# Second attention of a two-block transformer kernel: units of a head pair and a query half, matmuls that alternate between halves of the array, distances and maximum in one vector operation

## What is computed

```
N_HEADS, N_KV_HEADS, HEAD_DIM, WINDOW, BLOCK = 16, 4, 64, 128, 128
def sliding_window_attention(h, w_qkv, b_qkv, sinks, w_o, b_o):
    qkv = h @ w_qkv + b_qkv
    ...
    kb, vb = with_prev(k), with_prev(v)          # the block before and the own block
    scores = einsum("bnqgrd,bnkgd->bngrqk", q, kb) * HEAD_DIM ** -0.5
    dist = qi + BLOCK - kj
    valid = (dist >= 0) & (dist < WINDOW) & (key_pos >= 0)
    scores = where(valid, scores - slopes * dist, -inf)
    m = maximum(max(scores, -1), sink)
    p = exp(scores - m)
    probs = p / (sum(p, -1) + exp(sink - m))
    out = einsum("bngrqk,bnkgd->bnqgrd", probs, vb)
    return out.reshape(B, S, Q_DIM) @ w_o + b_o
```

## Time and profile before

| | |
|---|---|
| median of three runs | 2310.18 us |
| span of the profiled execution | 2305.6 us |
| median less span (no time of its own is listed for the profiled execution beside its span) | 4.6 us |
| TensorE busy | 2259.3 us, 98% |
| VectorE, GpSimd, ScalarE busy | 1151.5, 1049.4, 1000.7 us |
| second attention, first logits to the stage's tail | 132.64 us |
| granted TensorE clock in it | 1.00 |

### The profile page before, as it was taken

How to read it: one execution, slowest core, us unless ns; L and a number is a source line. 1 busy time by engine, 2 the same in 40 slices (tenths; PEclk the granted TensorE clock), 3 DMA queues, 4 the chain that set the end, 5 groups by cost and what they waited for, 6 DMA issues and landing times.

```text
span 2305.6 us, 28989 instructions
## 1 busy us (share of the span) xinstructions
PE 2259.3 (98%) x11624; PEld 1883.2 (82%) x11624; DVE 1151.5 (50%) x1766; ACT 1000.7 (43%) x1888; POOL 1049.4 (46%) x794
## 2 busy tenths in 40 slices
PE   7999999999999999999999999999999999999998
PEld 4788777778988888888888888878888889888887
DVE  4877787746522123377573335451543456724353
ACT  4765567654533224555552222463332236322234
POOL 2544443446444445522354454544354344544543
PEclk9999999999999999999999999999999999999999
DMA  6222233465232222311222222322222222232221
GB/s 281 92 84 100 89 134 126 163 216 186 75 110 92 92 106 90 121 41 38 74 92 99 98 96 92 110 92 92 78 105 92 92 92 74 92 109 82 101 103 62
DMA packets 42662, 239.79 MB, mean 104 GB/s; under 512 B 5024, under 2 KB 7072, under 8 KB 17184
## 3 DMA queue, kind: packets, MB, share of 16 engines
q1 hardware_dynamic: 40096, 232.28, 28.0%
q10 hardware_dynamic: 2432, 5.66, 0.8%
HBM read 226.38 MB, written 8.39 MB: 102 GB/s over the span
## 4 chain that ended last, share of the span: by engine, by line
PE 79%; DVE 11%; ACT 6%; POOL 2%; issue 1%; DMA 1%; ACTq 0%; DVEq 0%; SPq 0%; POOLq 0%
PE PS L739 78%; DVE DD L1881 2%; POOL WL L2622 1%; DVE TG L1887 1%; DVE HLO L1887 1%; DVE SQ L1887 1%; DVE PS L1887 1%; ACT WH L1309 1%; DVE X L1881 1%; DVE SCT L2204 1%; PE PS L1157 1%; DVE VV L1884 0%; DVE SB L2258 0%; ACT SB L1635 0%; DVE T L1881 0%
## 5 line engine op out<-in xcount | busy, mean ns | idle before, releaser
L2622 POOL TENSOR_TENSOR WL<-RAW,WH 128x512 fp32r<-128x512 f32 (+1 forms) x688 | 921.3, 1367 | 1122.0 <-ACT WH L1309 1105.0
L739 PE MATMUL PS<-HHI,WH 128*128 128x512 f32 x1488 | 595.4, 400 | 1.5 <-DVE GB L1887 1.4
L739 PE MATMUL PS<-HHI,WL 128*128 128x512 f32 x1488 | 580.6, 390 | 0.0
L739 PE MATMUL PS<-HLO,WH 128*128 128x512 f32 x1488 | 580.1, 390 | 0.0
L1309 ACT ACTIVATE WH<-RAW 128x512 fp32r<-128x512 f32 (+1 forms) x688 | 378.3, 613 | 394.7 <-PE PS L739 375.8
L739 PEld LDWEIGHTS PS<-HHI,WH 128*128 128x128 f32 x1488 | 279.8, 188 | 74.1 <-issue 12.6
L739 PEld LDWEIGHTS PS<-HHI,WL 128*128 128x128 f32 x1488 | 279.5, 188 | 59.4
L739 PEld LDWEIGHTS PS<-HLO,WH 128*128 128x128 f32 x1488 | 280.0, 188 | 56.6 <-issue 2.2
L739 PE MATMUL PS<-UF,WH 128*128 128x512 f32 (+1 forms) x832 | 224.0, 357 | 0.0
L1881 DVE TENSOR_TENSOR T<-PS,R 128x512 f32<-128x512 f32 x112 | 76.9, 690 | 217.8 <-PE PS L739 209.9
L739 PEld LDWEIGHTS PS<-UF,WH 128*128 128x128 f32 x832 | 148.3, 189 | 22.8
(11 more groups left out here) (357 smaller groups left out, 3574.7 us busy)
## 6 DMA issues: line engine op xcount, KB each, us to landing
RAW<-in_wts SPq DMA_DIRECT2D x190, 1024.0 KB, 4.9
FW<-in_wts SPq DMA_DIRECT2D x6, 1024.0 KB, 17.4
spill<-T SPq DMA_DIRECT2D x24, 256.0 KB, 3.4
RAW<-in_wts SPq DMA_DIRECT2D x8, 768.0 KB, 4.1
GT<-spill SPq DMA_DIRECT2D x20, 256.0 KB, 4.3
X<-in_xt SPq DMA_DIRECT2D x2, 1024.0 KB, 9.2
out_x<-X SPq DMA_DIRECT2D x8, 256.0 KB, 2.3
X<-in_xt SPq DMA_DIRECT2D x2, 768.0 KB, 9.0
```

Of the source, the lines that this page charges most:

```text
L739: return e.matmul(o_, l, r, start=start, stop=stop)
L2622: return e.tensor_tensor(o_, a, b, f)
```

## The change

A unit u is now head pair k = u // 2 and query half u % 2 (blocks 0 and 1, or 2 and 3), for both heads of the pair, i = 0 and 1. There are again 16 units, and the two buffers, banks and turns are used as before.

- Logits: for each block and each part the matmul of head i = 0 (partitions 0-63, bank 0) is followed by that of head i = 1 (partitions 64-127, bank 1). Block 0's missing previous block is left out, so an even unit has 6 matmuls and an odd one 8.
- Values: likewise i = 0 (output partitions 0-63) and i = 1 (64-127) in turn, 6 or 8 matmuls.
- Queries are scaled by -1 / (8 slope), `QUERY[h]` = -2^((h+1)/2 - 3), when their bias is added (a new constant qf; bq is multiplied by it once), so that one table of distances, DW [256], serves all heads. One `tensor_tensor_reduce` per head and block adds DW, scales and takes the maximum: four of 128x256, or two of 128x256 and two of 128x128 in an even unit. The sinks are negated once; one small operation gives the negative maximum, a second the exponent of the sink, `sink2`.
- Order on TensorE: logits of h+1, values of h-2, transposes of h-1, the pieces of `ROUNDS[h]`; values of 15 after the loop. The copies out of bank 4 and into O2 move one turn later too.

The core of the diff:

```diff
-        def logits2(h):
-            g, r0 = h // 4, 64 * (h % 2)
...
+        def logits2(u):
+            k, g = u // 2, u // 4
...
+            for nn in range(2):
+                n = 2 * (u % 2) + nn
+                for part, kb in ((0, n - 1), (1, n)):
+                    for i in range(2):
+                        if kb >= 0:
+                            r, c0 = slice(64 * i, 64 * i + 64), 256 * nn + 128 * part
+                            t = mm(PS[:, i, c0:c0 + 128], Q2[r, k, 128 * n:128 * n + 128], K2[r, g, 128 * kb:128 * kb + 128], True, True)
...
+                    for i in range(2):
+                        if kb >= 0:
+                            t = mm(PS[64 * i:64 * i + 64, 4, 128 * n:128 * n + 128], V2[:, kb, 64 * g:64 * g + 64],
+                                   PT[:, 4 * part + 2 * nn + i, :], part == 0 or n == 0, part == 1)
...
         for h in range(17):
-            n = len(ROUNDS[h])
+            if h < 15:
+                logits2(h + 1)
+            if h > 1:
+                values2(h - 2)
             if h:
                 turn2(h - 1)
-            if h < 15:
-                logits2(h + 1)
-                n = 0
-            for s in ROUNDS[h][:n]:
+            for s in ROUNDS[h]:
                 rows2(*s)
-            if h:
-                values2(h - 1)
-            for s in ROUNDS[h][n:]:
-                rows2(*s)
+        values2(15)
...
-                e.activation(Q2[:, k, :], Q2[:, k, :], ACT.Identity, bias=v("bq", k)).then_inc(*up("a_mix", ("q2", k)))
+                q.wait_ge(*at(("bq",)))
+                e.activation(Q2[:, k, :], Q2[:, k, :], ACT.Identity, scale=v("qf", k), bias=v("bq", k)).then_inc(*up("a_mix", ("q2", k)))
...
-            stt(S[:, :, :], DW[:, :, :], -8.0 * 2.0 ** (-8.0 * (h + 1) / 16), pv, MUL, ADD).then_inc(*up("d_ev", ("logits2_ev", h)))
-            q.wait_ge(*at(("logits2_ev", h)))
-            e.reduce_max(C2(h, 0), S[:, :, :], AX).then_inc(*up("d_mix", ("max2", h)))
...
+            for i in range(2):
+                for nn in range(2):
+                    s, lo = 2 * nn + i, 128 if u % 2 == 0 and nn == 0 else 0
+                    t = e.tensor_tensor_reduce(S[:, s, lo:256], PS[:, i, 256 * nn + lo:256 * nn + 256], DW[:, lo:256],
+                                               1.0 / QUERY[u // 2 * 2 + i], -1e38, ADD, MAX, C2(u, s, 1))
+                t.then_inc(*up("d_ev", ("logits2_ev", u, i)))
...
-            if h:
-                o2_low(h - 1)
+            if h > 1:
+                o2_low(h - 2)
```

More of the change, by code:

```diff
@@ L74 @@
     [(0, 1), (2,), (3,)] + [(0,), (1,), (2,), (3,)] * 2 + [(0, 1), (2, 3), ()] + [(0, 1), (2,), (3,)])]
+QUERY = [-2.0 ** ((h + 1) / 2 - 3) for h in range(16)]
 STEPS["sgu"] = [s for s in STEPS["sgu"] if s[:2] not in (("in", 5), ("dn", 4), ("dn", 5))] \
@@ L1151, in turn2 @@
+            t.then_inc(*up("psum", ("logits2", u)))
+            for i in range(2):
+                holds(i, ("logits2_ev", u, i))
+        def turn2(u):
+            S = S2[u % 2]
+            q.wait_ge(*at(("weights2", u)))
             free(2)
             free(3)
[L1153 to L1164, removed]
+            for part in range(2):
+                for s in range(4):
+                    if part or u % 2 or s > 1:
+                        t = e.transpose(PS[:, 2 + part, 128 * s:128 * s + 128], S[:, s, 128 * part:128 * part + 128], ident)
+            t.then_inc(*up("psum", ("turn2", u)))
@@ L1165, in values2 @@
+            holds(2, ("pt", u))
+            holds(3, ("pt", u))
+        def values2(u):
+            g = u // 4
+            q.wait_ge(*at(("pt", u)))
             q.wait_ge(*at(("ev", U["v", 0], 1)))
             free(4)
-            for n in range(4):
+            for nn in range(2):
+                n = 2 * (u % 2) + nn
                 for part, kb in ((0, n - 1), (1, n)):
-                    if kb >= 0:
-                        t = mm(PS[r0:r0 + 64, 4, 128 * n:128 * n + 128], V2[:, kb, 64 * g:64 * g + 64], PT[:, 2 * n + part, :],
-                               part == 0 or n == 0, part == 1)
@@ new lines, in tops2, with weights2 @@
+            q.wait_ge(*at(("logits2_ev", u, 1)))
+            q.wait_ge(*at(("sinks",)))
+            stt(C2(u, 4).rearrange("p (a b) -> p a b", a=2), C2(u, 0).rearrange("p (a b) -> p a b", a=2), -0.125, sinks, MUL, MIN).then_inc(
+                *up("d_mix", ("top2", u)))
+            q.wait_ge(*at(("top2", u)))
+            tt(C2(u, 12).rearrange("p (a b) -> p a b", a=2), C2(u, 4).rearrange("p (a b) -> p a b", a=2), sinks, SUB).then_inc(
+                *up("d_mix", ("sink2", u)))
+        def weights2(u):
+            S = S2[u % 2]
+            q.wait_ge(*at(("p2", u)))
+            tt(C2(u, 16), C2(u, 8), C2(u, 12), ADD).then_inc(*up("d_mix", ("den2", u)))
+            q.wait_ge(*at(("den2", u)))
+            e.reciprocal(C2(u, 16), C2(u, 16)).then_inc(*up("d_mix", ("inv2", u)))
+            q.wait_ge(*at(("inv2", u)))
+            for s in range(4):
+                x = S[:, s, 128 if u % 2 == 0 and s < 2 else 0:256]
+                t = ts(x, x, C2(u, 16 + s, 1), None, MUL)
+            t.then_inc(*up("d_mix", ("weights2", u)))
@@ L2864 @@
     dw = np.where((dd >= 0) & (dd < 128), dd, far).astype(f)
-    dw0 = dw.copy()
-    dw0[:, :128] = far
-    distw = np.concatenate([dw0, dw, dw, dw], axis=1)
+    distw = dw
     wst = I["sgu_w_s_2"][0].transpose(2, 0, 1).reshape(128, 1024)
```

121 lines of the change are left out of this document (52 added, 69 removed).

## The result

The kernel after took 2278.74 us, median of four runs (2277.32 to 2279.20). Four runs of the kernel before beside it gave 2310.55 (2308.28 to 2311.75). The ratio is 0.9864, with a 95% interval of 0.9852 to 0.9876: 31.8 us faster. The forecast was 2282.5, 3.8 too high.

The account below looks back on a forecast made before the run. TensorE's queue was taken to bound the second attention. Its stretch was to be 132.6 - 28.1 (halves) - 0.6 (start wait) + 1.0 (collisions) = 104.9 us, the time 2310.2 - 27.7 = 2282.5, range 2279 to 2290.

Parts of the forecast that it names:

- Logits 1.01 less, values 0.75 less, times 16: 28.1: Second attention on TensorE: alternating halves and fewer records save 1.76 us per unit, 28.1 us over 16 units.
- Weight loads of column halves are hidden: Values on TensorE: column-half pairs pay no extra for loads, taken from scan rows at 0.060 us per pair.
- the rival of 2287.3: Values on TensorE: each pair pays 0.05 us more for unhidden weight loads, 4.8 us in all; chance 0.06.
- The array changes its shape as often as before, so the fixed parts stay: TensorE cycle: three shape changes before and after, fixed 0.30 us for logits and 0.25 for values unchanged.
- The start wait, 0.6: At 991 us TensorE waits for ScalarE's first copy PT; values one turn later remove that 0.6 us.
- The new operation steps by 0.33 and 0.20: VectorE's distances-and-maximum operation: 0.33 us for 256 columns and 0.20 for 128, mean 1.19 per unit.
- The loop of softmax: 4.97 against 5.63: VectorE and ScalarE loop per unit: 4.97 us against TensorE's 5.63, leaving a distance of 0.66.
- The third rival: Softmax loop becomes the bound: one 1.3 us GpSimd meeting in each of 11 turns, 7.0 us, 2288.5; chance 0.13.
- the bank of values: Next thing late for TensorE: the bank emptied by VectorE's copy, ending about 0.6 us before TensorE returns.
- Collisions, 1.0: VectorE operations meeting GpSimd in the stage: two or three meetings that stick out, charged 1.0 us.
- That the halves don't run side by side (2306): Logits and values on TensorE: no overlap in this order, 3.6 + 0.6 us saved at most; chance 0.04.
- that it gets slower (2316.5): Softmax loop of 8.8 us, new operation at 0.60 and two meetings per turn: 35 us lost against 28.7; chance 0.02.

Follow-up runs that it names:

- wide_logits: Kernel after, with logits by one matmul of 256 key columns per head and block instead of two of 128: 2279.48 us, ratio 0.9873.
- both_single: Kernel after, with logits and values of a unit ordered head by head, all of one half before the other: 2293.00 us, ratio 0.9926.
- values_soon: Kernel after, with the old turn order: transposes, logits of h+1, values of h-1, copies a turn earlier again: 2282.58 us, ratio 0.9881.
- two_ops: Kernel after, with distances and maximum in two VectorE operations per head and block instead of one, queries not scaled: 2291.42 us, ratio 0.9918.
- after_again: The kernel after, run again without an edit: 2279.84 us, ratio 0.9868.
- before_again: The kernel before, run again without an edit for a second profile: 2311.01 us (one run).
- pad_long: Kernel after, plus the long added operation: an unread VectorE maximum over 960 columns per unit, ahead of the weights: 2297.11 us, ratio 0.9950.
- pad_short: Kernel after, plus the short added operation: an unread VectorE maximum over 256 columns per unit, ahead of the weights: 2283.28 us, ratio 0.9887.

## Why the prediction was right, and where its numbers were off

*TensorE bounds, and each unit costs what its queue needs.* Right. TensorE has no idle time from 977.46 to 1080.74.

*Logits 1.01 less, values 0.75 less, times 16: 28.1.* Right. Over all 16 units the medians are 0.87 and 1.09 for logits (forecast 0.86 and 1.08) and 0.81 and 1.03 for values (0.81 and 1.03), against 1.98 and 1.67: 1.00 and 0.76 less, times 16 28.1. The step of a pair is (1.09 - 0.87)/2 = 0.11, and wide_logits shows that columns set it. That it comes from alternating and not from the smaller count of records is shown by both_single, which keeps the count and loses 12.9. What it does not lose is the missing block's 3.6 and, read from its stretches and not from a run without any overlap, 11.5 of TensorE's own look ahead.

*Weight loads of column halves are hidden* (against the rival of 2287.3). The values' 16 records step by 0.109 a pair, with two loads in each. The rival's extra 0.05 a pair is not there. The Trainium skill ("TensorE: Matmul & The Clock Gate", Part 3, The mechanism) has the rule that loads overlap only when the row group differs; this trace, at 0.109, does not agree.

*The array changes its shape as often as before, so the fixed parts stay.* Nearly. 7 transposes took 0.855 us ahead of logits; 6 and 8 take 0.63 and 0.85 now ahead of the projection, mean 0.74. In 14 of the 16 units that is 0.115 less, in the last two, whose transposes stood ahead of the projection before too, nothing: 1.5 in all. The pieces of projection became 0.05 to 0.09 longer a turn, 0.9 in all. The net is 0.6 us that the sum didn't have. It is the order that does it: in values_soon, with alternating halves and the old order, the transposes are at 0.75 and 0.97 (mean 0.86) again.

*The start wait, 0.6.* Right in size (0.68, against the medians of other turns), wrong in its reason. The prediction has it go because the values move one turn back; in values_soon they don't, and of the wait 0.1 is left. By ScalarE's rows it is the softmax ending earlier that took it away; no run changes that alone.

*The new operation steps by 0.33 and 0.20.* Right: 0.34 and 0.21.

*The loop of softmax: 4.97 against 5.63.* This is the step that failed, without a cost in time. The room was taken as 0.66 and is 0.1 to 0.2 in the mean by the two added operations. The small operation ahead of the exponentials (L1891) takes 1.03 to 1.28 us in seven of the 16 units, three in a row at first and from then on every second one until 1042, against 0.17 when it meets nothing; I had counted 0.23 and a meeting here and there. In all seven it ends 0.02 us after an operation of GpSimd. Without the meeting the two turns would be 5.27 and 5.88 - 0.86 = 5.02, mean 5.15, an estimate that is near the forecast. The meeting comes every two turns for a reason that can be read in the trace: the operation that GpSimd has in hand follows ScalarE's WH, and this follows the copy of PT, for which ScalarE waits for TensorE's transposes:

```profile
1006.64 1.03 ACT L1797 ACTIVATE PT<-PS 128x1024 f32<-128x1024 f32 x1 [0.96 <-PE PS L1160]
1007.57 0.62 ACT L1311 ACTIVATE WH<-RAW 128x512 fp32r<-128x512 f32 x1
```

GpSimd's WL then ends at 1009.55 and the small operation at 1009.57. So the loop is tied to TensorE's cycle by that meeting. TensorE waits for none of it, but the added operations show how little is left. The third rival had this mechanism with 1.3 us in every turn; it is 0.86 in every second. VectorE's whole work was put at about 4.1 us a unit and is 4.9. And what comes late first was to be the bank of values: with more work in the loop it is the logits' banks, in eight waits of nine with the long operation; only in two_ops does the bank of values come in as often.

*Collisions, 1.0.* Not paid: no wait of TensorE for VectorE is listed in the stage; only its weight loads wait, 1.4 us in four times, while its matmuls still run.

*The sum.* 28.1 + 0.6 + 0.7 is 29.4, which is what was measured. The forecast for the stage was 104.9 and it is 103.3: 1.0 of that is the charge for collisions, 0.6 the shapes. The 4.6 us "around" the span cancel, as the forecast starts from the median. Another 1.2 us was won outside the stage, around 1540, where TensorE's matmuls and loads waited for WL before and do not after; after_again has it too, before_again does not. Waits there in the kernel before, for matmuls:

```profile
PE PS L739 <- POOL WL L2622: 0.6, 2, 0.3
```

GpSimd starts that WL earlier in the kernel after. In its queue stands ahead of it an operation on WS, which waits for the transfer of WS: issued at the same distance from the tail, it lands after 3.4 us where it took 4.9 in both profiles of before (and 4.4 in wide_logits). Why it lands sooner was not settled. The stage's 1.6 and this 1.2 make 2.8 of the 3.8 us; the last 1.0 is less than four runs of one kernel lie apart (1.9), and isn't explained.

*The other rivals.* That the halves don't run side by side (2306) and that it gets slower (2316.5) are both out: with the new operation at 0.34 and not 0.60 the loop stayed far below the 8.2 us from which that rival decides.

## What to carry to other kernels

When TensorE is the bound and its matmuls use half of its rows or half of its columns, bring two independent streams, one for each half, and keep their matmuls within a few of each other; strict alternation is best, groups of four records cost 0.05 to 0.10 us a stretch, and long groups lose about half of the gain. Before the gain is booked, follow the loop of the other engines at its real durations beside GpSimd: here the shorter TensorE cycle left it 0.1 to 0.2 us of margin, and without the cheaper maximum 10.8 of the 29.4 us would have been lost again. A longer stage of one profile is read against that stage in another, not through the whole time, where 3.7 us of scatter lay ahead of it; and its granted clock is read first, or 5 us of slower clock pass for the cost of an edit, as they nearly did with the long operation. A list of waits that is empty does not say that nobody waits: in values_soon the start of the values 0.05 us after the copy, in every turn, is the sign.

## What was not expected of the hardware

- TensorE starts matmuls of the other half before all those ahead of them in program order have started: the second half's first record at 1002.150 in both_single, beside the third of six of the first half.
- A 128x4 operation of VectorE with two inputs in SBUF takes 0.16 us when it meets nothing and up to 1.28 when GpSimd's 1.3 us operation is running, and then ends 0.02 us after it; with GpSimd fed through TensorE's own cycle, the meeting returns every two turns.
- The same 8 transposes take 0.85 us ahead of full-width matmuls and 0.97 ahead of the logits' 64-row ones.
- TensorE's granted clock fell to its lower level for 3.4 us three times in pad_long's stage, each time within 0.6 us of the end of a TensorE wait of 2.2 to 2.6 us; with waits of at most 1.4 (pad_short) or 1.0 (two_ops) it stayed at 1.00.
